# S5 Toeplitz matmuls in four column strips of TensorE, with one PSUM bank per half

## The reference

```python
def s5_mixer(u, a_re, a_im, log_dt, b_re, b_im, c_re, c_im, d, h0):
    ...
    a_bar = jnp.exp(lam_dt)
    b_bar = ((a_bar - 1.0) / lam)[..., None] * lax.complex(b_re.astype(F32), b_im.astype(F32))
    bu = jnp.einsum('blgc,gpc->blgp', uf.astype(jnp.complex64), b_bar)
    a_seq = jnp.broadcast_to(a_bar, bu.shape)
    _, h = lax.associative_scan(_linear_combine, (a_seq, bu), axis=1)
    ...
    y = jnp.real(jnp.einsum('gcp,blgp->blgc', c, h)) + d.astype(F32).reshape(S5_GROUPS, S5_GROUP) * uf
```

## Time and profile before

| | value |
|---|---|
| runs (median of 3) | 1655.92 us (1654.31 to 1656.34) |
| profiled execution, its own time | 1657.92 us |
| span of the profiled execution | 1656.0 us |
| PE busy | 1594.0 us, 96% of the span |
| PEld busy | 1354.8 us, 82% |
| DVE, ACT, POOL busy | 46%, 26%, 9% |
| mean granted TensorE clock | 0.99 |

### The profile page before, as it was taken

The page is one execution under the profiler, slowest core; times in us unless marked ns, Lnnn a source line. Parts: engine busy times, 40 slices in busy tenths (PEclk is TensorE's granted clock), DMA queues, the critical chain, the costliest instruction groups (busy, mean ns, idle before and its releaser), DMA issues.

```text
span 1656.0 us, 20670 instructions
## 1 busy us (share of the span) xinstructions
PE 1594.0 (96%) x8006; PEld 1354.8 (82%) x8006; DVE 761.5 (46%) x2248; ACT 424.8 (26%) x1151; POOL 146.7 (9%) x260
## 2 busy tenths in 40 slices
PE   7999799999999999999999999999999999999998
PEld 5888698787778788888888888978787878888887
DVE  3968963455665421551117497516556642111001
ACT  2123143533242222100001332353423322111001
POOL 0004700000120000000000074000003000000000
PEclk9999999999999999999999999999999999999999
DMA  9433414276366347544444343324844844444441
GB/s 273 133 92 124 129 52 127 64 226 203 114 202 205 128 156 176 144 146 134 152 135 146 102 144 115 101 89 137 263 129 141 229 140 142 152 142 150 153 151 53
DMA packets 293684, 239.74 MB, mean 145 GB/s; under 512 B 31870, under 2 KB 292590, under 8 KB 293374
## 3 DMA queue, kind: packets, MB, share of 16 engines
q1 hardware_dynamic: 208816, 197.89, 39.1%
q10 hardware_dynamic: 84772, 40.55, 8.9%
HBM read 217.69 MB, written 20.99 MB: 144 GB/s over the span
## 4 chain that ended last, share of the span: by engine, by line
PE 79%; DVE 13%; DMA 4%; ACT 2%; issue 1%; ACTq 1%; DVEq 0%
PE psum L542 52%; PE psum L860 14%; DMA out_new_ret_s<-arena 3%; DVE arena L1672 2%; PE psum L566 2%; ACT arena L902 2%; PE psum L621 1%; PE psum L640 1%; PE psum L623 1%; PE psum L604 1%; DVE arena L1678 1%; PE psum L606 1%; DVE arena L1519 1%; DVE arena L1597 1%; PE psum L510 1%
## 5 line engine op out<-in xcount | busy, mean ns | idle before, releaser
L542 PE MATMUL psum<-arena 128*128 128x264 f32 x4864 | 1110.9, 388 | 5.0 <-DVE arena L1844 5.0
L542 PEld LDWEIGHTS psum<-arena 128*128 128x128 f32 x4864 | 921.4, 191 | 170.6 <-DVE arena L1844 6.6
L902 ACT ACTIVATE arena<-psum 128x264 f32<-128x264 f32 (+14 forms) x490 | 191.7, 414 | 457.7 <-PE psum L542 290.4
L860 PE MATMUL psum<-arena 128*128 128x264 f32 x1024 | 229.6, 385 | 0.0
L860 PEld LDWEIGHTS psum<-arena 128*128 128x128 f32 x1024 | 193.7, 189 | 34.9
L1672 DVE SCALAR_TENSOR_TENSOR arena<-arena 128x128 f32<-128x128 f32 x256 | 71.6, 352 | 71.2 <-ACT arena L902 71.2
L1892 DVE SCALAR_TENSOR_TENSOR arena<-psum,rstd 128x264 f32<-128x264 f32 x64 | 27.5, 433 | 160.0 <-PE psum L542 159.8
L1905 DVE TENSOR_TENSOR arena<-arena,psum 128x264 f32<-128x264 f32 x16 | 6.9, 431 | 197.4 <-PE psum L860 197.4
L902 ACT ACTIVATE arena<-psum,arena 128x128 f32<-128x128 f32 x256 | 69.6, 387 | 67.7 <-DMA out_new_ret_s<-arena 55.0
L902 ACT ACTIVATE arena<-arena 128x264 f32<-128x264 f32 x32 | 16.5, 517 | 262.6 <-DVE arena L1905 219.8
L1311 ACT ACTIVATE arena<-arena 128x264 f32<-128x264 f32 x64 | 27.1, 425 | 190.4 <-DVE arena L1892 187.0
(11 more groups left out here) (236 smaller groups left out, 1296.0 us busy)
## 6 DMA issues: line engine op xcount, KB each, us to landing
arena<-in_w_in SPq DMA_DIRECT2D x80, 1024.0 KB, 5.3
arena<-in_w_mlp_up SPq DMA_DIRECT2D x32, 1024.0 KB, 5.4
arena<-in_w_mlp_down SPq DMA_DIRECT2D x32, 1024.0 KB, 5.1
arena<-in_w_s_out SPq DMA_DIRECT2D x16, 1024.0 KB, 5.4
arena<-in_state_ret ACTq DMA_DIRECT2D x16, 512.0 KB, 5.4
out_new_ret_s<-arena ACTq DMA_DIRECT2D x16, 512.0 KB, 7.3
arena<-in_state_ssd ACTq DMA_DIRECT2D x16, 512.0 KB, 4.4
arena<-in_w_ret_out SPq DMA_DIRECT2D x8, 1024.0 KB, 5.2
```

The source lines that it names most:

```text
L542: mm = pe.matmul(banks[b % 4][:, 0:TOK], ring[:, c, k, (b % 2) * P:(b % 2) * P + P], rhs[:, k, :], start=(k == 0), stop=(k == 7))
L860: mm = pe.matmul(banks[(2 * j + b) % 4][:, 0:TOK], ring[:, c, k, b * P:(b + 1) * P], hid[:, 8 * c + k, :], start=(c == 0 and k == 0), stop ...
L902: return nc.scalar.activation(out, in_, ACT.Copy, scale=scale)
```

## The change

The 32 matmuls of a half keep their operands and their shapes. Their outputs are placed differently. Pair 4i+j now goes to partitions 32j to 32j+31 (column strip j of the array, given by `tile_position`) and to columns 128i to 128i+127 of one bank. Before, all outputs went to partitions 0 to 31, and each i had a bank. The order is now: for each i, the real matmuls of the four strips, then the imaginary ones. One fill K{hf} replaces four, so there is one `bank_filled` at the end of the batch. ScalarE's 16 shifted copies go strip by strip and read from partitions 32j; the destination is `toep[..., j:16:4, ...]`.

```diff
-        + [f for hf in range(2) for f in ([f"K{hf}{i}" for i in range(4)] + [f"Y{hf}{i}" for i in range(4)])]
+        + [f for hf in range(2) for f in ([f"K{hf}"] + [f"Y{hf}{i}" for i in range(4)])]
...
                         pe.wait_ge(s["e_ready"], hf + 1)
+                        o = open_fill(f"K{hf}")
                         for i in range(4):
-                            nm = f"K{hf}{i}"
-                            o = open_fill(nm)
-                            for j in range(4):
-                                lm = 4 * i + j
-                                pe.matmul(o[0:32, j * P:(j + 1) * P], bblk[:, 0, lm, :],
-                                          eb[:, 0, lm, 0:4, :].rearrange("p a b -> p (a b)"), start=True, stop=False)
-                                mm = pe.matmul(o[0:32, j * P:(j + 1) * P], bblk[:, 1, lm, :],
-                                               eb[:, 1, lm, 0:4, :].rearrange("p a b -> p (a b)"), start=False, stop=True)
-                            close_fill(mm, nm)
+                            for ri in range(2):
+                                for j in range(4):
+                                    lm = 4 * i + j
+                                    mm = pe.matmul(o[32 * j:32 * j + 32, i * P:(i + 1) * P], bblk[:, ri, lm, :],
+                                                   eb[:, ri, lm, 0:4, :].rearrange("p a b -> p (a b)"),
+                                                   start=(ri == 0), stop=(ri == 1), tile_position=(0, 32 * j))
+                        close_fill(mm, f"K{hf}")
...
-                            drained(pe, f"K{hf}{i}")
+                            if i == 0:
+                                drained(pe, f"K{hf}")
...
-                        for i in range(4):
-                            filled(act, f"K{hf}{i}")
-                            src = bank(f"K{hf}{i}")[0:32, :].rearrange("p (j c) -> p j c", j=4)
+                        filled(act, f"K{hf}")
+                        for j in range(4):
+                            src = bank(f"K{hf}")[32 * j:32 * j + 32, :].rearrange("p (i c) -> p i c", i=4)
                             for r in range(LIFT):
-                                ins = copy(toep[32 * r:32 * r + 32, 4 * i:4 * i + 4, 32 * r:P], src[:, :, 0:P - 32 * r])
-                            is_drained(ins, f"K{hf}{i}")
+                                ins = copy(toep[32 * r:32 * r + 32, j:16:4, 32 * r:P], src[:, :, 0:P - 32 * r])
+                        is_drained(ins, f"K{hf}")
...
-                            for i in range(4):
-                                filled(act, f"K1{i}")
+                            filled(act, "K1")
```

## The result

The changed kernel took 1629.31 us (median of 4 runs, 1627.85 to 1631.92) against 1656.13 us (1654.31 to 1656.38) for the kernel before on the same chip. The ratio is 0.9842, with an interval of 0.9825 to 0.9859.

A forecast was written before the change was run, and what follows sets the result against it. PE was taken as the bound, busy for 96% of the span. Three full-clock batches (15.6 us) and the first batch (4.1) made 19.7 us, so 1655.92 became 1636.2 us, with a range of 1633.0 to 1642.5.

The forecast's parts named there:

- What bounds the kernel: Whole kernel: PE, busy 96% of the span, so time leaving its stream leaves the total unless another engine holds it.
- What the strips do: Toeplitz batches: four strips overlap fully, 64 passes in 16 waves of 0.11 us, 1.92 us a batch at full clock.
- the first rival: Toeplitz batches: waves take twice as long, 3.65 us a batch, 13.8 us saved in all, 1642.1 us; chance 0.13.
- Three batches at full clock: First layer's second batch and both of the second layer: each from 7.11 to 1.92 us, together 15.6 us saved.
- the wait for the sorting: Behind a second half's outputs: PE's 3.7 us wait for ScalarE's sorting (7.4 us in 2) moves along with the outputs.
- The first batch: First layer's first batch, at the low clock: outputs start at 224.9 instead of 229.03, 4.1 us gained.
- the new wait: First layer, before the first half's outputs: PE waits about 1 us for VectorE's scan.
- The sum of the batches: All four Toeplitz batches: 15.6 + 4.1 = 19.7 us saved.
- The edits that cost nothing: Single fill, fewer waits, another bank for the K fills: no cost, with DMAs and their order untouched.
- The clock: PE's low-clock stretches behind idle times may come or go: 2.7 us allowed to either side.
- PE's issue as the bound: Toeplitz batches: issue at 0.062 us a pass makes a batch 4.1 us, 13.1 us saved, 1642.8 us; chance 0.12.
- A price for each change of strip: Toeplitz batches: 0.065 us for each of 31 strip changes, without overlap, 8.1 us slower in all, 1664.0 us; chance 0.04.

The follow-up runs named there:

- the repeated median: The changed kernel, unaltered, measured again in more rounds with another profile: 1633.03 us (1628.04 to 1635.53).
- the nine executions together: All nine executions of the unaltered changed kernel, over its several measurements: median 1630.3 us.

## Why the prediction was wrong in size, point by point

- **What bounds the kernel**: right. Time that left PE's stream left the total, and no other engine took its place.
- **What the strips do**: right. Full overlap, 1.88 us for 1.92 forecast, and two strips 3.61 for the 3.65 of the first rival. The price of two strips carried over to four. The Trainium skill's rule against it ("TensorE: Matmul & The Clock Gate", Part 3, on packing) does not hold for column strips here: with the loads of each wave in the open a batch would be 3.65 us by the estimate of the first rival, and it is 1.88.
- **Three batches at full clock**: 5.22 each for 5.2. ScalarE's copies, 7.52 for 7.50, moved along, and the wait for the sorting stayed (7.4 us in 2).
- **The first batch**: 4.06 (5.40 less 1.34) for 4.1. The batch came out at 3.57 us for the forecast 3.6, the new wait at 1.1 for 1.
- **The sum of the batches**: 19.7 for 19.7.
- **"The edits that cost nothing"** is the step that failed. I counted "fewer waits" at nothing, and said that DMAs and their order are not touched. Their order is not; the moment of one is. Taking the waits out moved ScalarE's issue of one store by 0.27 us in the second layer. Put back alone they cost 4.9 us at that place, taken out alone they give 4.6; by medians 2.0 to 5.7 and 3.0 us. With 19.7 this makes 24.3, and 1631.8 us, below the range. Against the repeated median that is 1.2 off, against the first 2.5, against the nine executions together 1.5. The page had a sign of it: 4% of the chain that ended last, some 66 us, was DMA, and I did not ask what PE waited for there.
- **The clock**: I allowed 2.7 us to either side for low stretches that come or go. That was their size, but it was the only allowance. The rest of the difference, from 24.3 to 26.8, is of that size too, and no run shows what it is beyond such differences between executions. It is not the first layer's store: that gave 4.15 us in the pair of profiles, but it was waited for in one execution of three of either kernel, and the changed kernel with that wait took 1628.83 us, less than its two profiled executions without it (1630.33 and 1635.53).
- **The rivals**: none held. Passes at twice the distance and PE's issue as the bound are excluded by 1.88 us for 64 passes, 0.027 us a pass against the 0.062 read from the transposes. The figure of about 62 ns per MATMUL in the Trainium skill ("TensorE: Matmul & The Clock Gate", Part 1) does not bound this batch either. A price for each change of strip is excluded by 31 changes in 1.88 us.

What stays open is why four instructions fewer on ScalarE make one of its issues 0.27 us earlier. Open is also why a store is longer when a 1 MB load starts 0.05 us behind it than at 0.3, and what decides in the first layer between 0.3 and 2.0.

## What to carry to other kernels

Small matmuls whose stationary has 32 columns can share the array four at a time, and here 64 float32 passes then took the time of 16, if the strips alternate in the program; written strip by strip the same passes gained only 1.2 us of these 5.2 a batch. Before a wait or an instruction is counted at nothing, look for DMAs that the engine issues close to those of another queue: if the chain of waits goes through their landing, a few tenths of a microsecond decided over several here. And idle time of PE that is filled is only gained if the clock stays up behind what is left of it, which it did not in the one try here.

## What the runs showed of the hardware

- Four column strips of float32 matmuls run at once with no loss that can be seen: 64 passes with their 64 loads in 1.88 us, 256 in 7.20.
- PE starts passes of a free strip ahead of waiting ones, but does not reach far: order alone made a batch 1.88, 1.96 or 5.89 us.
- A store of 512 KB with a 1 MB load issued 0.02 to 0.05 us behind it took 9.0 to 9.7 us, and 4.8 to 6.7 us with the load 0.3 us or more behind, in the same layer; in the first layer it took 6.8 to 8.9 us at 0.33 and 5.0 to 6.6 at 2.0.
- From 1.3 us after the end of a 2.5 us wait the granted clock was 0.50 for 20.5 us of unbroken work, the longest such stretch in any of these profiles. Behind waits of 2.3 and 2.8 us it was 3.4 us, and behind the one of 1.1 us in the changed kernel there was none.
